# Hybrid attention block on eight cores: inputs stored in load order, another order of the first loads, one range fold for both rotary tables, rotary products as rows of their own

## The reference

```
mod = silu(c) @ ada_w + ada_b                 # six vectors: sh1, sc1, ga1, sh2, sc2, ga2
h = rmsnorm(x, ln_mix_g) * (1 + sc1) + sh1
q_lat, kv_lat, k_rope, q_s, k_s, v_s, gl_a, gl_b = split(h @ w_in)
y_mla: q = rmsnorm(q_lat) @ w_uq (8 heads, 64 plain + 32 rotary), k, v from rmsnorm(kv_lat) @ w_ukv,
       k gets one rotary part of 32 shared by the heads; causal softmax over all tokens
y_swa: 16 query heads on 2 key heads, window 128, relative bias, a sink in the softmax
x = x + ga1 * ((sigmoid(gl_a + b) * (y_mla @ w_o_mla) + sigmoid(gl_b + b) * (y_swa @ w_o_swa)) @ w_o)
h = rmsnorm(x, ln_mlp_g) * (1 + sc2) + sh2
x = x + ga2 * (relu(h @ w_ff1)**2 @ w_ff2)
return rmsnorm(x, ln_final_g)
rotary: t1*cos - t2*sin, t1*sin + t2*cos, angle = position * inv
```

## Time and profile before

| | us |
|---|---|
| median of 3 runs | 1395.92 |
| lowest, highest | 1393.61, 1542.28 |
| profiled execution, its own time | 1395.63 |
| its span, slowest core | 1394.0 |
| spans of the eight cores | 1389.4 to 1394.0 |
| TensorE busy | 1283.1 (92%) |
| VectorE, ScalarE, GpSimd busy | 632.3, 655.7, 201.4 |
| bytes read from memory, written | 127.15 MB, 8.41 MB |

### The profile page before, as it was taken

One profiled execution on the slowest core, in us unless ns is written; L12 is line 12 of the kernel. 1 busy time (PEld: TensorE's weight loads), 2 busy tenths in 40 slices (PEclk: granted clock), 3 DMA queues, 4 the chain that ended last, 5 costly groups with the idle time before them and its releaser, 6 DMA issues.

```text
span 1394.0 us, 20354 instructions; the slowest of 8 cores (1389.4 to 1394.0 us)
## 1 busy us (share of the span) xinstructions
PE 1283.1 (92%) x7010; PEld 587.4 (42%) x7010; DVE 632.3 (45%) x860; ACT 655.7 (47%) x901; POOL 201.4 (14%) x174
## 2 busy tenths in 40 slices
PE   0778889999999899999999999999999999999996
PEld 0533444444444353232444444444444444444442
DVE  2578665666662114324222222664443443443356
ACT  0387778979889716849322222443003103202333
POOL 3000435220035101000233322010000000000000
PEclk9999899999999999999999999999999999999999
DMA  9982754130353205020442524386214204000014
GB/s 168 215 110 41 152 119 102 46 62 1 61 73 86 40 1 54 1 27 1 130 44 27 54 31 61 122 115 98 31 14 78 31 1 79 13 1 1 1 61 181
DMA packets 95250, 88.20 MB, mean 63 GB/s; under 512 B 36768, under 2 KB 79824, under 8 KB 95056
## 3 DMA queue, kind: packets, MB, share of 16 engines
q0 software_dynamic: 72640, 51.03, 27.3%
q1 hardware_dynamic: 22512, 35.89, 8.0%
HBM read 127.15 MB, written 8.41 MB: 97 GB/s over the span
## 4 chain that ended last, share of the span: by engine, by line
PE 81%; ACT 7%; issue 4%; DVE 3%; DMA 3%; SPq 1%; ACTq 0%; DVEq 0%; POOL 0%; another core or an unknown queue 0%; POOLq 0%
PE psb L452 81%; ACT arena L457 7%; DMA arena<-eoh 1%; SPq L275 1%; DVE arena L461 1%; DMA scr<-arena 1%; DVE arena L477 1%; DVE arena L473 1%; DMA arena<-xo 1%; DVE arena L469 0%; DVE arena L466 0%; ACTq L314 0%; DVEq L314 0%; ACT L457 0%; POOL arena L461 0%
## 5 line engine op out<-in xcount | busy, mean ns | idle before, releaser
L452 PE MATMUL psb<-arena 128*128 128x512 bf16 (+7 forms) x7010 | 1283.1, 343 | 99.9 <-ACT arena L457 34.4
L452 PEld LDWEIGHTS psb<-arena 128*128 128x128 bf16 (+4 forms) x7010 | 587.4, 100 | 795.3 <-issue 265.6
L457 ACT ACTIVATE arena<-psb 128x1024 bf16<-128x1024 f32 (+5 forms) x479 | 370.6, 822 | 124.5 <-PE psb L452 121.5
L457 ACT ACTIVATE arena<-psb,arena 128x512 f32<-128x512 f32 x220 | 150.7, 687 | 461.5 <-PE psb L452 396.1
L461 DVE TENSOR_TENSOR arena<-psb,arena 128x512 f32<-128x512 f32 (+4 forms) x228 | 148.0, 661 | 321.9 <-ACT arena L457 217.2
L461 DVE TENSOR_TENSOR arena<-arena 128x512 bf16<-128x512 f32 (+2 forms) x176 | 128.9, 732 | 143.7 <-ACT arena L457 136.3
L457 ACT ACTIVATE arena<-arena 128x512 f32<-128x512 f32 (+3 forms) x196 | 137.9, 716 | 104.6 <-DVE arena L473 69.6
L473 DVE SCALAR_TENSOR_TENSOR arena<-psb,arena 128x512 f32<-128x512 f32 x160 | 120.2, 751 | 138.7 <-PE psb L452 137.9
L477 DVE CAST arena<-psb 64x512 bf16<-64x512 f32 (+1 forms) x126 | 86.8, 689 | 119.4 <-PE psb L452 117.9
L461 POOL TENSOR_TENSOR arena<-arena 128x512 bf16<-128x512 f32 (+1 forms) x56 | 97.5, 1741 | 200.5 <-DVE arena L461 185.9
L473 DVE SCALAR_TENSOR_TENSOR arena<-arena 128x512 bf16<-128x512 f32 (+5 forms) x106 | 80.8, 769 | 4.4 <-ACT arena L457 1.8
(11 more groups left out here) (14 smaller groups left out, 28.9 us busy)
## 6 DMA issues: line engine op xcount, KB each, us to landing
arena<-w_ff POOLq DMA_DIRECT2D x16, 1024.0 KB, 12.0
arena<-ada_w POOLq DMA_DIRECT2D x12, 1024.0 KB, 14.3
arena<-xo SPq DMA_DIRECT2D x16, 512.0 KB, 4.2
arena<-xo SPq DMA_DIRECT2D x4, 2048.0 KB, 9.3
out<-arena SPq DMA_DIRECT2D x16, 512.0 KB, 2.8
arena<-xo POOLq DMA_DIRECT2D x4, 1024.0 KB, 32.3
arena<-xs POOLq DMA_DIRECT2D x4, 1024.0 KB, 32.5
arena<-xs SPq DMA_DIRECT2D x8, 512.0 KB, 4.2
```

The lines of the kernel that those rows point to most:

```text
L452: S.op("pe", lambda e: e.matmul(out, lhsT=lhsT, rhs=rhs, start=start, stop=stop), reads=R, writes=Wr, sig=sig, cost=cost_of("pe", out, lhsT))
L457: S.op("act", lambda e: e.activation(out=out, in_=in_, func=func, **kw), reads=R, writes=Wr, cost=cost_of("act", out))
```

## The change

1. **Layouts.** All large inputs and the output are stored on the host so that each load is one contiguous run for each partition (16 KB in f32 for the 1 MB pieces). x is stored by groups of 512 tokens. The f32 loads of 1024 tokens for `ho` now have runs of 2 KB. A merge piece is one DMA.
2. **Order of the first loads** on POOL: pieces 2 and 3 (scale), the first x, pieces 0 and 1 (shift), then three x.
3. **Tables.** The loop over both columns, with its eleven instructions for each, is gone: one fold for both tables; the angle is folded in turns, sine and cosine come from two ScalarE calls with a scale and an offset. `tabO` holds cosine and signed sine in 32-row strips side by side.
4. **Rotary rows.** The products with cosine and with sine are rows of their own of the queries (64 rows), written by one instruction for each head; keys hold the rotated key twice, so a score matmul contracts 128 rows. The second copy, and those for the second head, come by three DMAs of 32 KB for each group. The rotary key block has 64 columns (latent weights 448 columns). One `stt` on 64 partitions takes the place of two on 32.
5. **Balance.** VectorE squares half of each own group too (ScalarE before).
6. **Planner.** Loads at 190 GB/s (POOL) and 370 GB/s (SP), first byte at 5 us, short plain loads slower, small matmuls and `ts` cheaper; a query step counts 1.4 for 2.6.
7. **Halo.** `late_loads` one column block later, two of the four later blocks do two halo steps.

```diff
@@ planner
-            own = tasks[i]["cost"] + tasks[i]["bytes"] / 180e3
+            own = tasks[i]["cost"] + tasks[i]["bytes"] / (190e3 if tasks[i]["e"] == "pool" else 370e3)
...
-        bw = 0.0
+        bw = 5.0
...
-                    done = done + 2.0 + t["bytes"] / 50e3
+                    done = max(done, 4.0) + 2.0 + t["bytes"] / 25e3
                 else:
-                    bw = max(bw, done) + t["bytes"] / 180e3
+                    bw = max(bw, done) + t["bytes"] / (190e3 if t["e"] == "pool" else 370e3)
...
-                return max(0.06, n / 2350.0) * (4 if ins[0].dtype == F32 else 1)
+                return max(0.03, n / 2350.0) * (4 if ins[0].dtype == F32 else 1)
@@ first loads
-        S.dma("sp", wkvxf, kc_src(win_d, 0, QC + KVC), "wkvx", writes=["wkvxf"])
+        S.dma("sp", V(o_wf, F32, 8 * (KVC + QC)), wlat_d, "wkvx", writes=["wkvxf"])
...
-        for i in range(4):
-            S.dma("pool", ada0[i], kc_src(adaw_d, 512 * i, 512 * i + 512), ("ada0", i), writes=[("ada0", i)])
+        def ada0_load(i):
+            S.dma("pool", V(o_ada0 + i * 8192, BF16, 8 * 512), adaw_d[i], ("ada0", i), writes=[("ada0", i)])
+        for i in (2, 3):
+            ada0_load(i)
...
-            S.dma("pool", xbs[i % NXB], src.rearrange("(kc p) n -> p kc n", p=128)[:, :, 512 * g:512 * g + 512],
+            S.dma("pool", V(o_xst + (i % NXB) * 8 * 512 * 2, BF16, 8 * 512), src[g].rearrange("p k n -> p (k n)"),
...
-        for i in range(NXB):
+        x_load(0)
+        for i in (0, 1):
+            ada0_load(i)
+        for i in range(1, NXB):
             x_load(i)
@@ tables
+        ts("dve", angt, posf, ropec[:, 0:1], None, ALU.mult, None, ["posf", "small"], ["angt"])
+        ts("dve", kf, angt, 1.0 / TWO_PI, None, ALU.mult, None, ["angt"], ["kf"])
+        cp("dve", posi, kf, ["kf"], ["kint", "posi"])
+        cp("dve", kf, posi, ["kint"], ["kf"])
+        stt(angt, kf, -CW1, angt, ALU.mult, ALU.add, ["kf", "angt"], ["angt"])
+        stt(angt, kf, -CW2, angt, ALU.mult, ALU.add, ["kf", "angt"], ["angt"])
+        ts("dve", kf, angt, 1.0 / TWO_PI, None, ALU.mult, None, ["angt"], ["kf"])
+        stt(posf, kf, 0.5, kf, ALU.is_gt, ALU.subtract, ["kf"], ["posf"])
+        stt(angt, posf, 0.5, posf, ALU.is_gt, ALU.subtract, ["posf"], ["angt"])
+        stt(kf, angt, 0.25, angt, ALU.is_gt, ALU.subtract, ["angt"], ["kf"])
...
-        for i in range(4):
+        for i in (2, 3, 0, 1):
             ada_mm(i, ada0[i], ("ada0", i))
@@ qr_build
-            tt("dve", rt1[HA, :], PS(pb)[HA, :], tabO[HA, cs], ALU.mult, [("ps", pb), ("tabO", 0)], ["rt1"])
-            tt("dve", rt2[HA, :], PS(pb)[HB, :], tabO[HB, cs], ALU.mult, [("ps", pb), ("tabO", 1)], ["rt2"])
-            for e in range(2):
+            for e, hs in ((0, HA), (1, HB)):
                 qt, qk = q_tile(j, e)
-                rs_ = slice(32 * e, 32 * e + 32)
-                tt("dve", qt[R2, cs], rt1[rs_, :], rt2[rs_, :], ALU.add, ["rt1", "rt2"], [qk + (g, 1)])
+                tt("dve", qt[HB, cs], PS(pb)[hs, :], tabO[hs, cs], ALU.mult, [("ps", pb), ("tabO", 0), ("tabO", 1)],
+                   [qk + (g, 1)])
@@ x_group
-            if own:
-                act(sq[:, 4:8, :], xb[:, 4:8, :], AF.Square, [xk], [("sq1", i % 2, 1)])
-            else:
+            if True:
                 tt("dve", sq[:, 4:8, :], xb[:, 4:8, :], xb[:, 4:8, :], ALU.mult, [xk], [("sq1", i % 2, 1)])
...
-            stt(rt1[R0, :], K_["t12"][R0, :], bvk[R0, 3:4], tab[R0, cs], ALU.add, ALU.mult,
-                [("t12", s_), "bvk", (tk, 0)], ["rt1"])
-            stt(rt2[R0, :], K_["t12"][R2, :], bvk[R2, 3:4], tab[R2, cs], ALU.add, ALU.mult,
-                [("t12", s_), "bvk", (tk, 1)], ["rt2"])
-            tt("dve", Kb[0][0][R2, ks], rt1[R0, :], rt2[R0, :], ALU.add, ["rt1", "rt2"],
-               [("Kpe0", 0, G)])
+            stt(rt1[HA, :], K_["t12"][HA, :], bvk[HA, 3:4], tab[HA, cs], ALU.add, ALU.mult,
+                [("t12", s_), "bvk", (tk, 0), (tk, 1)], ["rt1"])
+            tt("dve", Kb[0][0][R2, ks], rt1[0:32, :], rt1[32:64, :], ALU.add, ["rt1"], [("Kpe0", 0, G)])
+            for (e, p0) in ((0, 96), (1, 64), (1, 96)):
+                S.dma("sp", Kb[0][e][p0:p0 + 32, ks], Kb[0][0][R2, ks], ("kdup", G), reads=[("Kpe0", 0, G)],
+                      writes=[("Kdup0", G)], group=True)
@@ attention
-                mm(out, Kb[b][e][0:96, 128 * t:128 * t + 128], qt[0:96, 512 * c + qo:512 * c + 512], True, mk is None,
+                mm(out, Kb[b][e][:, 128 * t:128 * t + 128], qt[:, 512 * c + qo:512 * c + 512], True, mk is None,
...
-                steps.append(("Q", j, 0.44, 2.6, lambda j=j, g=g: qr_build(j, g, 7)))
+                steps.append(("Q", j, 0.44, 1.4, lambda j=j, g=g: qr_build(j, g, 7)))
...
-                if first and c == 0 and h == 6:
+                if first and c == 0 and h == 7:
                     late_loads()
...
-                    halo_step(2 * c + h % 2)
+                    for kc in {2: (0,), 3: (1,), 4: (2, 3), 5: (4, 5), 6: (6,), 7: (7,)}.get(2 * c + h % 2, ()):
+                        halo_step(kc)
```

More of the change, by code:

```diff
@@ L410, in build_program @@
     antiI_d = din("antiI", [128, 128])
-    out_d = nc.dram_tensor("out", [D, T], F32, kind="ExternalOutput").ap()
+    out_d = nc.dram_tensor("out", [4, 128, 8, 512], F32, kind="ExternalOutput").ap()
     scr_d = nc.dram_tensor("scr", [16, 384], F32).ap()
@@ L464, in ts @@
         def ts(eng, out, in0, s1, s2, op0, op1, R, Wr):
-            if s2 is None:
+            if eng == "dve":
+                n = 1
+                for x in out.shape[1:]:
+                    n *= x
+                S.op(eng, lambda e: e.tensor_scalar(out=out, in0=in0, scalar1=s1, scalar2=s2, op0=op0, op1=op1) if s2
+                     is not None else e.tensor_scalar(out=out, in0=in0, scalar1=s1, scalar2=None, op0=op0),
+                     reads=R, writes=Wr, cost=0.1 + 0.00061 * n)
+            elif s2 is None:
                 S.op(eng, lambda e: e.tensor_scalar(out=out, in0=in0, scalar1=s1, scalar2=None, op0=op0),
@@ L659, in build_program @@
         o_kvn = A.alloc(S_LEN * 2, 1, 3, "kvn")
-        o_K = [A.alloc(2 * S_LEN * 2, 1 + 2 * b, 3 + 0.5 * b, "K%d Kpe%d" % (b, b)) for b in range(2)]
+        o_K = [A.alloc(2 * S_LEN * 2, 1 + 2 * b, 3 + 0.5 * b, "K%d Kpe%d Kdup%d" % (b, b, b)) for b in range(2)]
         kvn = V(o_kvn, BF16, S_LEN)
@@ L934, in build_program @@
         ho_load(1)
-        for (b, e) in ((0, 1), (1, 0), (1, 1)):
-            S.dma("sp", Kb[b][e][R2, :], Kb[0][0][R2, :], ("kpe", b, e), reads=[("Kpe0", 0, G) for G in range(8)],
-                  writes=[("Kpe%d" % b, e, G) for G in range(8)] if (b, e) != (0, 0) else [])
+        for e in range(2):
+            S.dma("sp", Kb[1][e][HB, :], Kb[0][0][HB, :], ("kpe", e),
+                  reads=[("Kpe0", 0, G) for G in range(8)] + [("Kdup0", G) for G in range(8)],
+                  writes=[("Kpe1", e, G) for G in range(8)])
         def ada_piece(i):
@@ L1490, in _prep_common @@
         parts += [w_uq[:, h, 0:64] for h in pair]
-        parts += [w_uq[:, h, 64:96] for h in pair]
         for h in pair:
-            parts += [w_uq[:, h, 80:96], w_uq[:, h, 64:80]]
+            parts += [w_uq[:, h, 64:96], w_uq[:, h, 80:96], w_uq[:, h, 64:80]]
     wuq = np.concatenate(parts, axis=1)
@@ L1566 @@
         b, half = core // 2, core % 2
-        oT = np.asarray(res.results[core]["out"], np.float32)
+        oT = np.asarray(res.results[core]["out"], np.float32).transpose(2, 1, 0, 3).reshape(D, T)
         for lc, gc in enumerate(OWN_BLOCKS[half]):
```

135 lines of the change are left out of this document (64 added, 71 removed).

## The result

| | before | after |
|---|---|---|
| median of 3 runs, us | 1395.92 | 1418.09 |
| lowest, highest | 1393.61, 1542.28 | 1414.39, 1419.18 |
| ratio after/before, 95% interval | | 1.0153 [1.0132, 1.0173] |
| spans of the eight cores | 1389.4 to 1394.0 | 1408.0 to 1416.2 |
| mean start of the first exponential of the scores, all cores | 147.3 | 170.6 |

The kernel became some 22 us slower, not 35 faster. What comes after the projections did what was forecast.

What follows compares the result with a forecast made beforehand. Loads until 85 us, plus VectorE's range folds, were taken to delay the first score matmul; later TensorE is busy. Gains of 33 us there and 2 in attention made 1395.9 - 35 = 1361 us, range 1345 to 1380.

Steps and rivals of the forecast that it cites:

- first x lands at 27, second at 50: First loads: with casts at 5.2 us each, the first x lands at 27 us (before 52), the second at 50 (58).
- the loads don't get faster: Rival, chance 0.15: all casts stay at 6.7 us, second x at 59, gain 24 + 2, kernel 1370 us.
- The price from `w_ff2`: Casting loads with 4 KB runs cost 0.0053 of share per GB/s: 218 GB/s, 4.8 us at a share of 1.15.
- casts that still move 157 GB/s: Sign that the prediction is wrong: casting loads still move 157 GB/s at a full DMA share.
- from 11.8 where the positions have landed, to 23.5: VectorE's single range fold: 11.5 us of work starting when positions land, leaving VectorE free when the scale pieces land.
- VectorE waits past 40 us for a modulation add: Sign that the prediction is wrong: at the kernel's start, VectorE waits past 40 us for a modulation addition.
- Projections of the first group start at 28.: Projection stage: weights are scaled by 27 us, so first-group projections can start at 28 us instead of 55.
- VectorE is held by the late shift pieces: Rival, chance 0.17: VectorE waits until 45 us for pieces 0 and 1; first score at 124, gain 25 + 2, 1369.
- 53/0.80 = 66 us for seven groups: Projections after the second x: ScalarE's 53 us of work packed at 0.80 take 66 us; first score matmul at 116.
- the 33 us: Gain ahead of attention: the first score matmul starts at 116 us instead of 149.0, 33 us earlier.
- 2 us, 0 to 5: Attention: query builds lose 19.5 us of VectorE work; gain taken as 2 us, with 0 and 5 as ends.
- Clock at 128 rows: Rival, chance 0.03: 128-row scores lower attention's clock from 0.98; at 0.82 the kernel takes 1426 us.

Runs made afterwards that it cites:

- a5: The changed kernel with all four modulation pieces loaded and multiplied in the order 0, 1, 2, 3 ahead of x; 1414.5 us, ratio 1.0126.
- b1: The kernel before, with only the first four modulation pieces and the casting loads of x read from copies with 16 KB runs; 1426.4 us, ratio 1.0212.
- a3: The changed kernel with modulation pieces and x stored so that casting loads read 2 KB runs instead of 16 KB, same orders; 1402.1 us, ratio 1.0039.
- h2: The changed kernel with GpSimd's loads held until SyncE's latent weights and `eoh` have landed; about 1402 us, ratio 1.0051.
- h1: The changed kernel with GpSimd's loads held until latent weights and `eoh` land, and the four modulation pieces in order ahead of x; 1390.0 us, ratio 0.9960.
- a6: a3 (2 KB runs) with the modulation pieces 0, 1, 2, 3 ahead of x; 1398.3 us, ratio 1.0008.
- h3: h2 with the planner told that GpSimd's loads land from 14 us on and move 150 GB/s; 1393.6 us, ratio 0.9988.
- h4: h1 with the planner told that GpSimd's loads land from 14 us on and move 150 GB/s; 1395.2 us, ratio 0.9997.
- e1: a5 with four row-sum matmuls for eight, 7 us less TensorE work, norms wrong; 1413.4 us.
- e5: a5 with less work on TensorE (7 us), ScalarE (7) and VectorE (10) at once, norms wrong; 1409.5 us.
- g2: h1 with a shorter hold: GpSimd's loads wait for `eoh` alone, and the latent weights are issued behind it; 1385.8 us, ratio 0.9935.
- a1: The changed kernel with SyncE's seven small loads issued ahead of the positions and latent weights, orders of engines unchanged; 1415.3 us, ratio 1.0144.
- g1: h1 with modulation pieces and x in 2 KB runs, orders unchanged; 1402.7 us, ratio 1.0055.

## Why the prediction was wrong

*Loads: "first x lands at 27, second at 50".* Met (27.6, 52.1), for the wrong reason. The sum put positions (1.2 us) and latent weights (4.3) ahead of the casts at full speed and priced casts at 5.2. In fact a cast costs about 7 when alone (153 GB/s), as with 2 KB runs. For the first x this error was cancelled by the latent weights, which were pushed behind it (43.5); for the second by the table copies and `wukv`, priced at 7.4 ahead of it but issued only from 66 us. That was luck. Rival "the loads don't get faster" was nearer in the price, but its 1370 rests on the same wrong step. The price from `w_ff2` (0.0053 of share per GB/s) failed: a5's cast row has 0.0064, and the share reached 0.98, not the 1.15 of the sum. So the prediction's own sign, casts that still move 157 GB/s, came true.

*Fold: "from 11.8 where the positions have landed, to 23.5".* **The step that failed first.** It took SyncE's landings from the earlier trace rows and left them there, though the change altered the other queue's rows eightfold. Positions came at 18.1, `eoh` at 52.9; the fold ended at 63.7. I never listed what TensorE's first instruction waits for, though in the chain of waits of the kernel before it is the longest piece up to the scores, further up than the earlier trace rows. Nor was it harmless there, since the fold stood 12 us behind it:

```profile
11.36 18.42 DMA arena<-eoh
```

b1 and a3 show the step's price: +30 us and -16 us by the run length alone. The sign "VectorE waits past 40 us for a modulation add" came true as well (54.67), by this cause and not by that of the rival.

*"Projections of the first group start at 28."* They started at 68: 40 late.

*"VectorE is held by the late shift pieces" (1369).* Part of it is real, in another place: the block of f32 matmuls for the bias columns stood beside the loads before and stands between the first and second group now, 80.98 to 99.2, with ScalarE idle for 21 us. I wrote that TensorE's count of matmuls stays and never asked where they stand. Nor did the sum price what this block does to the clock. In after the granted clock falls behind these one-column matmuls:

```profile
80.00:100.00 20.00, 18.70 (x104) 13.86 (x101) 4.17 (x9) 2.48 (x3) 2.28 (x2) 0.56 0.43 79
```

```profile
100.09 0.18 PEld L455 LDWEIGHTS psb<-arena 128*64 128x64 bf16 x1 [0.25 <-issue]
100.52 0.18 PEld L455 LDWEIGHTS psb<-arena 128*64 128x64 bf16 x1 [0.25 <-issue]
```

The next products stand 0.43 us apart, 512 columns at 1.2 GHz, the lower of the clock's two levels. Over 80 to 112 us four cores were granted 0.63 to 0.68 and four 0.84; the first exponential stands at 172.2 on average on the former and at 169.0 on the latter. So about 3 us hang on how long it stays low. h2 was granted 0.50 or 0.51 from 60 to 80 us on all eight cores, h1 0.91 to 1.00: the lower level for 20 us, part of what the late pieces cost, though no run isolates it. Its net price has no fixed size: about 4 us in a5 and a6, 12 in h2 against h1, and none in h3 against h4 (1393.6 and 1395.2), where the planner knew the landings.

*Packing: "53/0.80 = 66 us for seven groups".* Wrong. Without any wait for x, a5's eight groups take 89 us: VectorE at 0.72, ScalarE at 0.66. Less work on the same chain of dependences only lowers the shares; e1 to e5 show it. TensorE, with 75 us the busiest of the three already in the earlier trace rows, was left out of the sum. So the 33 us did not come even with the starvation removed: the first exponential stands at 143.8 in h1 and 141.4 in g2, 3.5 and 5.9 us earlier than before. g2 lets the 57 us between forecast and measured time be split, as an estimate. Its second x landed at 57.1, 7 us after the 50 of the sum, and from there to the first exponential it took 84 us, 18 more than the 66. These two make the 25 us from 1361 to g2; the other 32, from g2 to after, are the starved loads and the late pieces.

*Attention: "2 us, 0 to 5".* Right in size: from the first exponential to the end 1244.0 became 1240.9, and it is 1239.2 to 1242.5 in all variants with the rotary rows but a1 (1245.4); b1, without them, has 1244.5. *Clock at 128 rows*: 0.98 as before. *Copies of the rotated key, merge pieces, halo: nothing*: no wait of TensorE on them in after. All later stages were shifted and not shortened, as forecast.

*The range, 1345 to 1380, and the rivals.* All cases but one lay under 1395.9, and the one above it was the clock. That the longer rows would hold up the other queue was no rival at all, and it decided the sign; the size of the stage decided that even the version without it gained 10 us and not 35.

## What to carry to other kernels

Two DMA queues on the same engines share by turns, packet for packet, not by bytes: before lengthening the rows of one, list the other queue's loads, the instruction that waits first for each, and what stands behind it in its engine's order. Count the short queue's rows, not its bytes. Several small inputs packed into one load of 128 rows should pay once for what they pay several times here; no run tried it. Long rows pay (12 us here) once the short loads are out of the way; holding the bulk queue for a few microseconds until they have landed turned 22 us of loss into 10 of gain (g2, with the pieces ahead of x). And a stage in which three engines are busy 0.66 to 0.84 by turns doesn't shrink with their sums: look for what stands between its first and last instruction.

## What the runs showed of the hardware

- Beside a casting queue with 16 KB rows, three loads of 128 short rows (24, 12 and 2 KB) took 11.3, then 6.7 and 6.3 us more (a1); with that queue held, the 24 KB took 3.6 from issue to landing (h1).
- Two busy queues moved equal counts of packets: 241 and 241, 1190 and 1190, 387 and 387.
- 128 KB table copies, issued twelve in a row: 7.0 us to landing beside 2 KB rows, 16.6 beside 16 KB rows.
- Issuing itself slows down: SyncE took 20 us over one 2 KB load in b1, where it took 0.43 in h1 (`hv`), and GpSimd 0.9 us for a cast of 2 KB runs against 0.55 of 16 KB.
- First products came from 56.6 to 64.8 us on the eight cores of g1, from 51.2 to 55.4 in h1; no run shows why.
- Fewer matmuls in the stage: a lower granted clock on all eight cores (e1, 0.89 to 0.92; a5, 0.96 to 1.00).

Open: why the planner's truer prices cost 5 us in h4, and which single dependence sets the 83 to 89 us of the stage, and what the lower clock behind the late pieces costs by itself. No run took the bias columns off the path altogether.
